# The last four experts of a mixture-of-experts layer: weights of three of them loaded as 4 MB pairs instead of 2 MB chunks

## The chip, the core and the metric

The kernel runs on one core of one Trainium2 chip. The metric is the device time of one execution in microseconds (us); where several executions are compared, their median. One more execution was taken with the hardware profiler: its span and its trace are what is read below.

## The reference

One encoder layer on 256 tokens of 1024 float32 values: a mixing stage (gated linear attention and grouped-query attention side by side), then a mixture of experts, and a final RMS norm. The change touches only how the expert weights come in:

```python
def moe_ffn(x, w_router, b_router, w1, b1, w2, b2):      # top-4 of 32 experts
    ...
    def expert_block(args):
        xb, e = args
        h = (xb @ w1[e] + b1[e]).astype(jnp.float32)      # 1024 -> 2048
        h_glu = jnp.minimum(h[:, :D_FF], SWIGLU_LIMIT)
        h_lin = jnp.clip(h[:, D_FF:], -SWIGLU_LIMIT, SWIGLU_LIMIT)
        act = (h_glu * jax.nn.sigmoid(SWIGLU_ALPHA * h_glu) * (h_lin + 1.0)).astype(xb.dtype)
        return act @ w2[e] + b2[e]                        # 1024 -> 1024
```

Each expert has 8 MB of w1 and 4 MB of w2 in float32, 12 MB in all, and all 32 are read: 384 MB out of 421 MB that the kernel moves.

## The kernel before

**Work.** The experts are taken in order, each for up to 64 of its tokens at a time. The weights of an expert come as six chunks of 2 MB, numbered r = 0 to 5 in the expert: four of w1 (two rows of 128 input features each, by 2048 columns) and two of w2. TensorE works through them in that order. For a chunk of w1 it issues 16 matmuls by the profile's count (line 1696), after the fourth it gathers the rows of the next expert (line 1588), adds the previous expert's result to the output banks (`combine`, line 1607), turns the hidden values (line 1724), the gates (line 1733) and the gathered rows (line 1596), and then does the two chunks of w2 (line 1742, 16 matmuls each) and the bias rows of the next expert (line 1517).

**The ring.** The chunks lie in a ring in SBUF of 8 slots of 2 MB. Both SP, which issues every load, and TensorE count chunks by the semaphore `chunk_used`: SP may load into a slot when the chunk that lay there has been used. All loads go down SP's one queue, in the order in which SP issues them. TensorE waits on a semaphore of the slot (`slot_in`), or of a pair of slots (`pair_in`), before the first matmul of what was loaded.

**Three ways of loading.** Chunks 0 to 71 (twelve experts) are loaded singly, 2 MB each (line 358, function `load`). From chunk 72 on they are loaded by pairs: one transfer of 4 MB into two neighbouring slots (line 401, `load_pair`). SP waits until both slots are free, and TensorE waits for the whole pair ahead of the first of its two chunks. Experts 16 to 27 are done by a loop of bodies of four experts (24 chunks). The last body, experts 28 to 31, is written out behind the loop. Its chunks are called u = 0 to 23 here, its experts q = 0 to 3. Before the change all its chunks are loaded singly again, and of its last expert the chunks r = 3, 4 and 5 (`FINE`) each in two pieces of 1 MB with a semaphore of their own (line 365, `load_pieces`).

**The end.** For the last expert, `last_hidden` turns the hidden values in two halves and does w2 by pieces (lines 1650 and 1656). After that come the last result (ScalarE, line 692), the last `combine`, the norm with `fin_g` (loaded at line 440 into slot 0, once chunk u = 18 has been used) and the stores.

Of the kernel before, what the change touches and what calls it, by code (L numbers as in the profile page):

```python
# [40 lines left out]
EXPERTS, TOP_K, FF = 32, 4, 1024  # L41
# [22 lines left out]
SLOTS = 8  # L64
# [11 lines left out]
FINE = (3, 4, 5)  # L76
# [5 lines left out]
UNROLL = 4  # L82
PER_BODY = UNROLL * PER_EXPERT
PAIR = 2
# [39 lines left out]
def encoder_layer(nc, x, w_in, w_out, w_router, w1, b1, w2, b2, gate_w, columns, rows, final_g,  # L124
                  c_keep, c_front, later, split, out):
    ctx = ExitStack()
    with ctx:
# [3 lines left out]
        def sem(name):  # L131
            return ctx.enter_context(nc.semaphore(name))
# [142 lines left out]
        S = type("Semaphores", (), {n: sem(n) for n in names})  # L275
        win_in = [sem(f"win_in{k}") for k in range(KD)]
        slot_in = [sem(f"slot_in{s}") for s in range(SLOTS)]
# [15 lines left out]
        def slot_of(c):  # L293

            return (c - OUTSIDE + TURN) % SLOTS

        def ring_slot(c):

            return (ring_chunks.index(c) + TURN) % SLOTS

        def earlier_halves(i):
            return sum(1 for o in SOON if o + SLOTS <= i and (o + TURN) % SLOTS == (i + TURN) % SLOTS)

        def slot(s):
            return ring[:, s * SLOT:(s + 1) * SLOT]
# [12 lines left out]
        def _(sp):  # L318
# [37 lines left out]
            def load(to, loaded, e, r):  # L356

                sp.dma_start(to, rows_of(e, r)[:, r % PAIR * SLOT:(r % PAIR + 1) * SLOT]).then_inc(loaded, 16)

            def load_pieces(to, e, r):  # L360

                for i in range(GROUPS):
                    n = SLOT // GROUPS
                    at = r % PAIR * SLOT + i * n
                    sp.dma_start(to[:, i * n:(i + 1) * n], rows_of(e, r)[:, at:at + n]).then_inc(piece_in[FINE.index(r) * GROUPS + i], 16)
# [37 lines left out]
            for i in range(SLOTS, len(ring_chunks)):  # L403
                c, s = ring_chunks[i], ring_slot(ring_chunks[i])
                if i - SLOTS in SOON:
                    e, r = divmod(c, PER_EXPERT)
# [16 lines left out]
            last = rounds * bodies + (bodies - 1)  # L423
            with sp.Fori(WRITTEN, last) as it:
                for u in range(0, PER_BODY, PAIR):
                    q, r = divmod(u, PER_EXPERT)
                    s = slot_of(u)
                    sp.wait_ge(S.chunk_used, it * PER_BODY + (u - SLOTS + PAIR))
                    load_pair(s, (it * UNROLL + q) % EXPERTS, r)
            for u in range(PER_BODY):  # L430
                q, r = divmod(u, PER_EXPERT)
                sp.wait_ge(S.chunk_used, last * PER_BODY + (u - SLOTS + 1))
                if q == UNROLL - 1 and r in FINE:
                    load_pieces(slot(slot_of(u)), EXPERTS - 1, r)
                else:
                    load(slot(slot_of(u)), slot_in[slot_of(u)], EXPERTS - UNROLL + q, r)
# [766 lines left out]
        def _(pe):  # L1203
# [30 lines left out]
            def xT(k, t=None):  # L1234
                return turned[:, k, :] if t is None else turned[:, k, t * P:(t + 1) * P]


            for k in range(KD):
# [4 lines left out]
                def put(o, l, r, first):  # L1243
                    return mm(o, l, r, start=a and first, stop=z, skip_group_check=True)  # L1244
# [3 lines left out]
                def keys_and_queries():  # L1248
                    for i, c0 in enumerate((C_GQ, C_GK)):
                        for pair in range(2):  # L1250
                            last = put(bank[MIX[i]][:, pair * SEQ:(pair + 1) * SEQ], w[:, c0 + pair * P:c0 + (pair + 1) * P], xT(k), pair == 0)
                    return last
# [4 lines left out]
                for banks, c0, c1 in ((ATT_A, C_ZG, C_TAIL), (ATT_B, C_TAIL, D_IN)):  # L1257
                    for t in range(TILES):
                        last = put(bank[banks[t]][:, 0:c1 - c0], xT(k, t), w[:, c0:c1], True)
                        if z:  # L1260
                            last.then_inc(S.pass1, 1)
                if not a:
                    last = keys_and_queries()
# [42 lines left out]
            for k in range(KD):  # L1306
                for t in range(TILES):
                    last = mm(bank[6 + t][:, :], xT(k, t), w_in_sb[:, k, C_GV:C_GR], start=k == 0, stop=k == KD - 1)  # L1308
# [303 lines left out]
            def nth_in_body(u):  # L1612

                return u // SLOTS + 1

            def loaded(q, r, it, final_body):

                u = q * PER_EXPERT + r
                if isinstance(it, int):
                    c = it * PER_BODY + u  # L1620
                    if c in EARLY:
                        i = EARLY.index(c)
                        pe.wait_ge(early_in[i], 16 if i < OUTSIDE - 1 else 16 * W1_ROWS)
                        return early[i] if i < OUTSIDE - 1 else early_rows
                    s = ring_slot(c)
                    if c < PAIRS_FROM:
                        pe.wait_ge(slot_in[s], (ring_chunks.index(c) // SLOTS + 1 + earlier_halves(ring_chunks.index(c))) * 16)
                    elif r % PAIR == 0:
                        pe.wait_ge(pair_in[s // PAIR], ((c - PAIRS_FROM) // SLOTS + 1) * 16)
                    return slot(s)  # L1630
                s = slot_of(u)
                if final_body:
                    singles = (PAIRS_FROM - 1 - OUTSIDE - (s - TURN) % SLOTS) // SLOTS + 1
                    singles += sum(1 for o in SOON if (o + TURN) % SLOTS == s)
                    pe.wait_ge(slot_in[s], (singles + nth_in_body(u)) * 16)
                elif r % PAIR == 0:
                    pe.wait_ge(pair_in[s // PAIR], (it * LOADS_PER_BODY + (nth_in_body(u) - PAIRS_FROM // SLOTS)) * 16)
                return slot(s)
# [38 lines left out]
            def expert(n, q, it, first=False, second=False, rows=None, final=False, final_body=False):  # L1677
# [7 lines left out]
                for c in range(W1_CHUNKS):  # L1685
                    if first and c == W1_CHUNKS // 2:
                        pe.wait_ge(S.xg_ready, 1)
                    fine = final and c in FINE
                    chunk = slot_for(q, c) if fine else loaded(q, c, it, final_body)
                    for r in range(W1_ROWS):  # L1690
                        k = c * W1_ROWS + r
                        if fine:
                            pe.wait_ge(piece_in[FINE.index(c) * GROUPS + r], 16)
                        for j in range(GROUPS):
                            for g in range(2):
                                last = mm(bank[(2, 5)[g]][j * CAP:(j + 1) * CAP, :], xg[:, k * CAP:(k + 1) * CAP],  # L1696
                                          of_group(row_of(chunk, r, 2 * FF), g, j), start=False, stop=k == KD - 1,
                                          skip_group_check=True)
                        if first and c in SOON and r == W1_ROWS // 2 - 1:
                            last.then_inc(S.half_used, 1)  # L1700
                    last.then_inc(S.chunk_used, 1)

                    if first and c == 0:
                        turn_first(1)
                    if first and c == 1:
                        turn_gates()
                    if rows:
                        rows(c)
# [29 lines left out]
                for s in range(W2_CHUNKS):  # L1738
                    chunk = loaded(q, W1_CHUNKS + s, it, final_body)
                    for r in range(W2_ROWS):  # L1740
                        for j in range(GROUPS):
                            last = mm(bank[6][j * CAP:(j + 1) * CAP, :], hidT[:, r, s * CAP:(s + 1) * CAP],  # L1742
                                      row_of(chunk, r, D)[:, j * 512:(j + 1) * 512], start=s == 0 and r == 0,
                                      stop=s == W2_CHUNKS - 1 and r == W2_ROWS - 1, skip_group_check=True)
                        if first and W1_CHUNKS + s in SOON and r == W2_ROWS // 2 - 1:
                            last.then_inc(S.half_used, 1)
                    last.then_inc(S.chunk_used, 1)
# [68 lines left out]
```

## Time and profile before

| | |
|---|---|
| median of 3 runs | 1043.68 us (1043.23 to 1044.42) |
| profiled execution, its time | 1042.15 us |
| its span | 1040.4 us |
| moved by DMA | 420.96 MB, mean 405 GB/s |
| TensorE busy | 998.6 us, 96% |
| VectorE, ScalarE busy | 220.2 us, 133.8 us |
| mean granted TensorE clock | 0.989 of full speed |

The span is what the trace covers; the execution's own time is 1.75 us longer. Matmuls overlap, so TensorE's busy share says little: what counts is when a group of matmuls starts, and what ended the idle time ahead of it. The granted clock has two levels, 1.00 (2.4 GHz) and 0.50 (1.2 GHz); a value between them is a mean over a stretch.

### The profile page before, as it was taken

To read this page: it belongs to the slowest core of one execution; us is meant where nothing else is said; L and a number is where in the kernel's file an instruction comes from. 1 tells how busy PE (TensorE), PEld (TensorE's weight loads), DVE (VectorE), ACT (ScalarE), POOL (GpSimd) and SP (SyncE) were. 2 spreads that over 40 slices of the span, in tenths; PEclk is the share of its full clock that TensorE was granted. 3 is DMA by queue.
4 is the path that set the end of the run, shared out by engine and by line. 5 is a ranking of instruction groups with operands and counts; after the bars stand their busy time and mean duration, and the time that the engine had idled before them with its cause. 6 is when DMAs were issued, how large, how long until landed. Compare 5 with 4: busy or idle time off the path is not lost.

```text
span 1040.4 us, 11246 instructions
## 1 busy us (share of the span) xinstructions
PE 998.6 (96%) x4709; PEld 425.0 (41%) x4709; DVE 220.2 (21%) x517; ACT 133.8 (13%) x267; POOL 12.3 (1%) x18
## 2 busy tenths in 40 slices
PE   9999999999999999989999989999999999999996
PEld 7656444444444444433333334333333333343332
DVE  2595341111111111101111111111111111011112
ACT  1164211111100001101111010001111011001112
POOL 0101000000000000000000000000000000000000
PEclk9999999999999999999999989999999999999999
DMA  9857889999999999999999999999999999999995
GB/s 335 239 220 312 363 312 430 426 428 426 428 428 427 427 428 428 431 433 431 430 430 433 430 431 430 430 431 433 432 433 431 428 433 432 427 426 428 427 424 228
DMA packets 27876, 420.96 MB, mean 405 GB/s; under 512 B 4480, under 2 KB 4992, under 8 KB 7584
## 3 DMA queue, kind: packets, MB, share of 16 engines
q1 hardware_dynamic: 27552, 420.15, 96.0%
q8 instruction: 29, 0.48, 0.2%
q10 hardware_dynamic: 288, 0.27, 0.1%
q14 instruction: 7, 0.06, 0.0%
HBM read 419.36 MB, written 1.05 MB: 404 GB/s over the span
## 4 chain that ended last, share of the span: by engine, by line
PE 64%; DMA 32%; DVE 2%; ACT 1%; issue 0%; SPq 0%; POOL 0%; POOLq 0%
DMA ring<-in_w_dram 32%; PE bank L1696 28%; PE bank L1742 14%; PE bank L1607 4%; PE bank L1244 3%; PE bank L1588 3%; PE bank L1492 1%; PE bank L1323 1%; PE bank L1724 1%; PE bank L1420 1%; PE bank L1596 1%; PE bank L1517 1%; PE bank L1656 1%; PE bank L1308 0%; PE bank L1733 0%
## 5 line engine op out<-in xcount | busy, mean ns | idle before, releaser
L1696 PE MATMUL bank<-ring,work 128*64 128x512 f32 x2000 | 453.5, 605 | 29.9 <-DMA ring<-in_w_dram 29.8
L1696 PEld LDWEIGHTS bank<-ring,work 128*64 128x64 f32 x2000 | 174.7, 138 | 288.8 <-issue 235.2
L1742 PE MATMUL bank<-ring,work 128*64 128x512 f32 x992 | 219.7, 595 | 0.2
L1124 DVE TENSOR_SCALAR work<-bank 128x512 f32<-128x512 f32 x31 | 21.4, 691 | 640.6 <-PE bank L1696 640.6
L1742 PEld LDWEIGHTS bank<-ring,work 128*64 128x64 f32 x992 | 68.7, 137 | 129.5 <-issue 124.5
L655 ACT ACTIVATE bank<-work 128x512 f32<-128x512 f32 x31 | 18.6, 601 | 495.6 <-DVE work L1124 495.6
L1607 PE MATMUL bank<-work 64*128 64x512 f32 x256 | 63.6, 615 | 0.7 <-ACT work L692 0.7
L1588 PE MATMUL bank<-h,work 128*64 128x512 f32 x248 | 60.0, 593 | 0.0
L668 ACT ACTIVATE work<-bank 128x512 f32<-128x512 f32 x31 | 18.5, 597 | 214.5 <-PE bank L1742 214.5
L1607 PEld LDWEIGHTS bank<-work 64*128 64x128 f32 x256 | 22.0, 186 | 41.8 <-issue 40.2
L1094 DVE TENSOR_TENSOR work<-bank,ffn_pairs 128x512 f32<-128x512 f32 x31 | 21.4, 691 | 72.2 <-PE bank L1596 72.2
L1588 PEld LDWEIGHTS bank<-h,work 128*64 128x64 f32 x248 | 23.5, 137 | 30.0 <-issue 30.0
L1724 PEld LDWEIGHTS bank<-ckeep,work 128*128 128x128 f32 x124 | 17.3, 209 | 24.7 <-DVE work L1130 23.2
L650 ACT ACTIVATE work<-bank 128x512 f32<-128x512 f32 x31 | 18.5, 597 | 46.8 <-DVE work L1130 43.6
L1724 PE MATMUL bank<-ckeep,work 128*128 128x128 f32 x124 | 23.2, 309 | 1.1 <-DVE work L1130 1.1
L1244 PE MATMUL bank<-ring,work 128*128 128x416 f32 (+1 forms) x64 | 22.9, 502 | 0.0
L660 ACT ACTIVATE work<-bank 128x512 f32<-128x512 f32 x31 | 18.5, 597 | 28.9 <-PE bank L1724 28.8
L1127 DVE SCALAR_TENSOR_TENSOR work<-work 128x512 f32<-128x512 f32 x31 | 21.5, 692 | 1.1
L1130 DVE TENSOR_TENSOR work<-work,bank 128x512 f32<-128x512 f32 x31 | 21.3, 687 | 1.1
L1125 DVE TENSOR_SCALAR work<-bank 128x512 f32<-128x512 f32 x31 | 21.1, 680 | 0.0
L1517 PE MATMUL bank<-biases,sel 96*64 96x512 bf16 x128 | 20.0, 389 | 0.0
L1596 PE MATMUL bank<-ckeep,work 128*128 128x128 f32 x124 | 20.0, 283 | 0.0
(218 smaller groups left out, 496.8 us busy)
## 6 DMA issues: line engine op xcount, KB each, us to landing
ring<-in_w_dram SPq DMA_DIRECT2D x48, 4096.0 KB, 30.0
ring<-in_w_dram SPq DMA_DIRECT2D x87, 2048.0 KB, 19.8
ring<-in_w_dram SPq DMA_DIRECT2D x12, 1024.0 KB, 20.6
ring<-in_w_in_dram SPq DMA_DIRECT2D x7, 1168.0 KB, 18.1
work<-in_w_dram SPq DMA_DIRECT2D x2, 2048.0 KB, 14.9
ring<-in_w_out_dram SPq DMA_DIRECT2D x2, 1024.0 KB, 10.2
ring<-in_w_out_dram SPq DMA_DIRECT2D x1, 2048.0 KB, 17.0
h<-in_x_dram SPq DMA_DIRECT2D x4, 256.0 KB, 6.4
```

The lines of the kernel that those rows point to most:

```text
L1094: nc.vector.tensor_tensor(xg.rearrange("p (h r c) -> p h r c", h=GROUPS, c=CAP), bank[2][:, :].rearrange("p (r h c) -> p h r c", h=GROUPS, ...
L1124: nc.vector.tensor_scalar(glu, bank[2][:, :], LIMIT, None, ALU.min).then_inc(S.glu_ready, 1)
L1127: nc.vector.scalar_tensor_tensor(lin, lin, 1.0, glu, ALU.add, ALU.mult).then_inc(S.dve_step, 1)
L1130: nc.vector.tensor_tensor(lin, lin, bank[2][:, :], ALU.mult).then_inc(S.hid_ready, 1)
L1244: return mm(o, l, r, start=a and first, stop=z, skip_group_check=True)
L1517: mm(bank[(2, 5)[g]][j * CAP:(j + 1) * CAP, :], sel, of_group(b1_parts, g, j), start=True, stop=False, skip_group_check=True)
L1588: last = mm(bank[6][j * CAP:(j + 1) * CAP, :], onehot[:, t, :], h[:, t, j * 512:(j + 1) * 512], start=t == 0, stop=t == TILES - 1, skip_gr ...
L1596: last = nc.tensor.transpose(bank[2][:, r * P:(r + 1) * P], apart[:, :, r], ident)
L1607: last = mm(bank[Y[i]][:, :], gatedT[j * CAP:(j + 1) * CAP, t, :], res[j * CAP:(j + 1) * CAP, :], start=start, stop=stop, skip_group_check ...
L1696: last = mm(bank[(2, 5)[g]][j * CAP:(j + 1) * CAP, :], xg[:, k * CAP:(k + 1) * CAP], of_group(row_of(chunk, r, 2 * FF), g, j), start=False ...
L1724: last = nc.tensor.transpose(bank[5][:, r * P:(r + 1) * P], apart[:, :, r], ident)
L1742: last = mm(bank[6][j * CAP:(j + 1) * CAP, :], hidT[:, r, s * CAP:(s + 1) * CAP], row_of(chunk, r, D)[:, j * 512:(j + 1) * 512], start=s = ...
```

## The change

For the first three experts of the last body (u = 0 to 17) SP now issues nine transfers of 4 MB instead of eighteen of 2 MB, each when both of its slots are free. TensorE waits for them by the pair's semaphore, ahead of the first chunk of each pair. The last expert (u = 18 to 23) is loaded as before: three single chunks and six pieces. Its count on `slot_in` is adapted, because fewer single loads go ahead of it. Bytes, order of the bytes, places in the ring and all computation stay as they are.

```diff
             for u in range(PER_BODY):
                 q, r = divmod(u, PER_EXPERT)
+                if q < UNROLL - 1:
+                    if r % PAIR == 0:
+                        sp.wait_ge(S.chunk_used, last * PER_BODY + (u - SLOTS + PAIR))
+                        load_pair(slot_of(u), EXPERTS - UNROLL + q, r)
+                    continue
                 sp.wait_ge(S.chunk_used, last * PER_BODY + (u - SLOTS + 1))
-                if q == UNROLL - 1 and r in FINE:
+                if r in FINE:
                     load_pieces(slot(slot_of(u)), EXPERTS - 1, r)
                 else:
                     load(slot(slot_of(u)), slot_in[slot_of(u)], EXPERTS - UNROLL + q, r)
@@
                 s = slot_of(u)
-                if final_body:
+                if final_body and q == UNROLL - 1:
                     singles = (PAIRS_FROM - 1 - OUTSIDE - (s - TURN) % SLOTS) // SLOTS + 1
                     singles += sum(1 for o in SOON if (o + TURN) % SLOTS == s)
-                    pe.wait_ge(slot_in[s], (singles + nth_in_body(u)) * 16)
+                    pe.wait_ge(slot_in[s], (singles + 1) * 16)
                 elif r % PAIR == 0:
                     pe.wait_ge(pair_in[s // PAIR], (it * LOADS_PER_BODY + (nth_in_body(u) - PAIRS_FROM // SLOTS)) * 16)
```

## Rows read from the trace of the kernel before

**Rows 1.** The page: span, and DMA rate in 40 equal slices.
```profile
span 1040.4 us, 11246 instructions
GB/s 335 239 220 312 363 312 430 426 428 426 428 428 427 427 428 428 431 433 431 430 430 433 430 431 430 430 431 433 432 433 431 428 433 432 427 426 428 427 424 228
```

**Rows 2.** The chain that ended last, from 960 us: start us, us, what.
```profile
978.94 34.01 DMA ring<-in_w_dram
...
1024.73 6.18 PE bank L1656 x28
```

**Rows 3.** Windows, loads by pairs and loads by singles: busy time, PEclk, DMA share, GB/s.
```profile
444.00:902.00 458.00, 432.06 (x1980) 168.34 (x1978) 69.02 (x156) 40.60 (x76) 0.00 (x0) 0.98 1.00 431
910.20:998.30 88.10, 85.12 (x407) 34.28 (x404) 16.32 (x36) 10.00 (x19) 0.00 (x0) 1.00 1.01 427
```

**Rows 4.** DMA issues from 850 us on: count, KB each, median us from issue to landing.
```profile
ring<-in_w_dram SPq DMA_DIRECT2D x3, 4096.0 KB, 31.4
ring<-in_w_dram SPq DMA_DIRECT2D x6, 1024.0 KB, 34.1
ring<-in_final_g_dram SPq DMA_DIRECT2D x1, 512.0 KB, 20.7
```

**Rows 5.** Timeline of SP's queue from 860 us: start us, us, what.
```profile
982.46 13.91 SPq L365 DMA_DIRECT2D ring<-in_w_dram  x6
1008.29 0.33 SPq L440 DMA_DIRECT2D ring<-in_final_g_dram  x1
```

**Rows 6.** Timeline of TensorE, last body: start us, us, what, [idle before <- releaser].
```profile
921.74 13.96 PE L1696 MATMUL bank<-ring,work 128*64 128x512 f32 x64
935.47 1.94 PE L1588 MATMUL bank<-h,work 128*64 128x512 f32 x8
...
983.65 3.70 PE L1696 MATMUL bank<-ring,work 128*64 128x512 f32 x16 [1.22 <-DMA ring<-in_w_dram]
988.53 3.70 PE L1696 MATMUL bank<-ring,work 128*64 128x512 f32 x16 [1.17 <-DMA ring<-in_w_dram]
...
997.23 7.09 PE L1742 MATMUL bank<-ring,work 128*64 128x512 f32 x32
...
1004.60 7.19 PE L1696 MATMUL bank<-ring,work 128*64 128x512 f32 x32
1012.99 7.14 PE L1696 MATMUL bank<-ring,work 128*64 128x512 f32 x32 [1.20 <-DMA ring<-in_w_dram]
```

**Rows 7.** Timeline of TensorE while the loads come by pairs.
```profile
461.86 7.14 PE L1696 MATMUL bank<-ring,work 128*64 128x512 f32 x32 [2.51 <-DMA ring<-in_w_dram]
...
608.86 10.07 PE L1696 MATMUL bank<-ring,work 128*64 128x512 f32 x32 [3.06 <-DMA ring<-in_w_dram]
...
842.25 7.14 PE L1696 MATMUL bank<-ring,work 128*64 128x512 f32 x32 [1.03 <-DMA ring<-in_w_dram]
...
854.39 7.09 PE L1742 MATMUL bank<-ring,work 128*64 128x512 f32 x32
...
861.77 7.11 PE L1696 MATMUL bank<-ring,work 128*64 128x512 f32 x32
871.39 7.14 PE L1696 MATMUL bank<-ring,work 128*64 128x512 f32 x32 [2.51 <-DMA ring<-in_w_dram]
...
900.53 8.83 PE L1696 MATMUL bank<-ring,work 128*64 128x512 f32 x32 [2.47 <-DMA ring<-in_w_dram]
...
914.37 7.09 PE L1742 MATMUL bank<-ring,work 128*64 128x512 f32 x32
```

**Rows 8.** The first reader of `fin_g`: durations in ns, first and last start in us.
```profile
L1175 DVE TENSOR_TENSOR tok<-bank,ring x2: 691/691/691, 1033.6 to 1034.6; 128x512 f32<-128x512 f32 x2
```

**Rows 9.** Windows behind three of those waits, columns as in rows 3.
```profile
608.00:614.70 6.70, 5.84 (x14) 1.89 (x16) 0.00 (x0) 0.00 (x0) 0.00 (x0) 0.50 1.01 435
871.40:875.00 3.60, 3.60 (x18) 1.47 (x20) 0.00 (x0) 0.00 (x0) 0.00 (x0) 1.00 1.01 437
901.60:904.80 3.20, 3.20 (x11) 0.86 (x8) 0.00 (x0) 0.00 (x0) 0.00 (x0) 0.50 0.98 420
```

## The prediction

> **What bounds the kernel now.** I read four views, in this order. The page first: from the seventh slice to the last but one, DMA moves 424 to 433 GB/s without a break [rows 1]. The windows say the same more sharply: the DMA engines are fully busy (share 1.00) while the loads come by pairs, and again in the last body, where they come singly [rows 3]. So up to the last loads the kernel goes at the pace of its weights. The reader is to see that this doesn't yet say what ends it. For that there is the chain of waits: it follows a transfer to 1012.95 us, and from there on it is TensorE, with the engines that follow it, until 1040.4 [rows 2]. The timeline of TensorE shows which transfer that is: at 1012.99 the matmuls of u = 20 start, the third chunk of the last expert, after 1.20 us of waiting for it [rows 6]. Of the six pieces behind u = 20 none is on the chain, though DMA is still moving them. The last pair of pieces was issued by 992.6 to 996.4 (the stretch of six issues ends there, the last one long) [rows 5], and by the median of 34.1 us they land around 1027 to 1030 [rows 4]; TensorE runs its 28 matmuls of w2 from 1024.73 in one go [rows 2], at a plain 0.22 us each, so none of them stands waiting.
>
> So the end is set by: landing of u = 20, or the moment when TensorE is done with u = 19, whichever is later, plus 1040.4 - 1012.99 = 27.4 us. Now it is the landing, and TensorE has 1.20 us to spare. That spare time is what the change must be weighed against.
>
> **The change, part by part.** *The transfers.* Six chunks by pairs take one period of the pair stage: TensorE's waits end at 842.25 and 900.53, two experts apart, so 58.28 / 2 = 29.14 us for an expert [rows 7]. Six single chunks take 1012.99 - 983.65 = 29.34 us (u = 14 to u = 20) [rows 6]. The same ratio is in the rates, 431 against 427 GB/s [rows 3]. For three experts that is 3 x 0.20 = 0.6 us, by which everything from u = 18 on lands earlier; u = 20 lands at 1012.95 - 0.6 = 1012.35. Nine issues fewer on SP cost nothing: SP sits waiting for free slots, with 30 us of work in the queue.
>
> The Trainium skill (DMA: Bandwidth & Descriptors, "Anatomy of one DMA — SWDGE (gpsimd) path") gives each transfer a fixed cost of about 2.0 us beside the time of its bytes. By that nine transfers fewer would be worth up to 18 us if they ran one by one, and the forecast would be faster. The trace does not agree for a full queue: 2 x 29.34 / 6 - 29.14 / 3 = 0.07 us a pair.
>
> *SP's wait.* A pair is issued when both slots are free, one chunk later than a single one; queued behind this wait are all later loads and `fin_g`. It costs nothing: a load lies about 31 us in the queue before it has landed, three times the 9.71 us (29.14 / 3) that a pair takes [rows 4], so the queue holds some 20 us of work at each issue. The pair stage, with this very wait, kept the engines at share 1.00 [rows 3]. If that cover were gone, the cost would be at most one chunk, 4.9 us, once.
>
> *TensorE's wait.* This is where I see the cost. With pairs TensorE may start u = 14 only when u = 15 has landed too. Now it starts u = 14 at 983.65 and u = 15 at 988.53, each on its landing, and by the time u = 15 is there only one chunk is left to do [rows 6]. With pairs both start at the landing of the pair. That is 900.53 + 3 x 29.14 = 987.95. (0.6 us ahead of 988.53, as it should be.) From there, all by start-to-start distances of undisturbed rows:
> - from the start of that pair to the first matmul of w2: 854.39 - 842.25 = 12.14 us [rows 7], so 1000.09. Now it is 997.23 [rows 6]: 2.86 us later. The w2 pair has landed long before, at 987.95 + 9.71 = 997.66;
> - from there to u = 18: 1004.60 - 997.23 = 7.37 [rows 6] (7.38 in the pair stage, 861.77 - 854.39 [rows 7]), so 1007.46. u = 18 has landed at about 1002.5;
> - u = 18 and 19 without a wait: half of 935.47 - 921.74 = 13.73 [rows 6], so 6.87, and u = 20 can start at 1014.33.
>
> u = 20 has landed by then (1012.35), and no wait is left: the 1.20 us are used up, and TensorE is late by 1014.33 - 1012.99 = **1.34 us**. The pieces behind come 0.6 us earlier and are asked for 1.3 us later, so they hold up nothing, and the tail is only shifted. `fin_g` is issued when u = 18 is used: 1008.29 now [rows 5], 2.9 us later then. It lands at 1029.0 [rows 4, 5]; shifted by the full 2.9 us it would be there at 1031.9, and its first reader starts at 1033.6 now [rows 8], at 1034.9 then. Everything in experts q = 0 and 1 is within the ring's slack: TensorE waits there in either kernel.
>
> Sum: +1.34. The span becomes 1040.4 + 1.3 = 1041.7, the profiled execution 1042.15 + 1.3 = 1043.5, and the median 1043.68 + 1.34 = **1045.0 us**. (The profiled execution lies 1.5 us under the median. I take the difference as the same for both.) That is +0.13%.
>
> *The clock.* With the pair wait at u = 14 TensorE stands idle ahead of it, and what the clock does there now counts in full, because nothing behind u = 14 waits for DMA any more. In the pair stage eight waits lasted 2.4 us or more, from the one that ended at 461.86 to that at 900.53. After five of them the clock fell to 0.50 (1.2 GHz), three not (the first and the last of the eight [rows 7]; two of the five and one of the three [rows 9]). The cost: from 900.53 to w2 13.84 us instead of 12.14, so 1.7 us; in the longest case, at 608.86, 10.07 instead of 7.14, 2.9 us [rows 7]. After a fall TensorE is late, and the wait of the next expert is short (about 1 us, as the 1.03 at 842.25), after which the clock never fell. So falls come in every second expert at most. The waits of 1.2 us that the kernel before has in its last body brought none, its windows are at 1.00 [rows 3].
>
> What happens at u = 14 (q = 2) then depends on the experts ahead. In this execution the clock fell at 900.53, so q = 0 would wait about 1 us, q = 1 about 2.6, and q = 2 about 1 (clock fell at q = 1) or 2.7. Another execution may stand the other way round. With a fall in five of eight long waits (0.63), and none after a fall, a wait is long in x = 1 - 0.63 x of the cases, so 0.61, and a fall just at u = 14 has 0.61 x 0.63 = 0.38. I cost it at nothing in the likeliest case, with 1.7 us as the other end (2.9 the rare extreme).
>
> The Trainium skill (TensorE: Matmul & The Clock Gate, "HAM oscillation — how this bites in real kernels") says that a wait for DMA between blocks of matmuls drops the clock to half and lets each next block start cold. By that the fall at u = 14 would be certain and the sum 1.34 + 1.7 = +3.0 us. The trace agrees on the price, and on the rule only in five of eight.
>
> **The rivals.**
> - *The clock falls at u = 14.* +1.34 + 1.7 = +3.0 us: 1046.7, slower by 0.29%. For it: five of eight such waits. Against it: the falls alternate, and a fall at q = 1 protects q = 2. It decides from a cost of 0.75 us on (2.09 - 1.34). Chance 0.36.
> - *The landing stays the bound.* The landing of a load is that of its slowest DMA engine. If that falls behind by 1 to 2 us in other executions late in the body, both kernels wait for u = 20 and only the 0.6 us of faster loads are seen: 1043.1. For it: the spare time is small. Against it: three waits in a row end at an even distance, 29.14 us twice (842.25, 871.39, 900.53) [rows 7]. A lag d between u = 15 and u = 20 gives 1.34 - d, down to -0.6 from d = 1.94 on. Chance 0.11.
> - *Loads by pairs are worth more than the rate says*, since the queue is served better. It would have to be 2 us or more in nine transfers, and the pair stage shows 0.6. Chance 0.02.
> - *The queue runs dry between pairs*, up to 4.9 us: 1048.6. Against it: share 1.00 over 458 us of pairs. Chance 0.01.
>
> **How the numbers follow.** A measurement of this kernel can tell about 0.2%, 2.09 us, from no change. The likeliest case, 0.50: TensorE late by 1.3 us, 1045.0, in a range of 1044.3 to 1045.7 (the three runs spread by 0.7 about their median). Same: 0.50 + 0.11 = 0.61, faster 0.02, slower 0.36 + 0.01 = 0.37. The range goes from the landing case (1043.1) to the case of the clock with that spread (1046.7 + 0.7): 1043.0 to 1047.4, outside it mainly the double-length fall (1047.9) and the dry queue.
>
> **What would show it.** Right: in the last body TensorE's groups of line 1696 come as x32 behind a wait; a wait that ends at about 988.0; line 1742 of q = 2 starts at about 1000.1, and from there to the end of line 1696 no wait for the ring at all, with the 1.20 us at u = 20 gone; u = 20 starts about 1014.3; the DMA rate of the last body 431 instead of 427 GB/s, and the last loads 0.6 us earlier. Wrong: a wait still standing at u = 20 (then the landing is the bound, and it may be faster), a clock of 0.50 behind 988 (then +3.0), or a DMA share under 1.00 between 910 and 1000.

## The result and the profile after

| | before | changed |
|---|---|---|
| median of 20 runs each | 1043.14 us (1042.12 to 1044.42) | 1044.66 us (1043.44 to 1046.84) |
| ratio of the times, changed to before, 95% interval | | 1.0019 [1.0013, 1.0025] |
| profiled execution: span, its time | 1040.4, 1042.15 us | 1044.3, 1046.02 us |

The changed kernel is slower by 0.19%, 2.0 us by the ratio and 1.5 us by the medians (the means, 1043.21 and 1045.07, are 1.9 apart). Median and mean differ because its 20 runs are not one heap. Twelve lie between 1043.44 and 1044.80 (median 1044.40, +1.26 us on the median of before), eight between 1045.80 and 1046.84 (median 1046.07, +2.9), and none between. No run of before lies above 1044.42. The profiled execution is one of the eight.

Its page has the same DMA rate as before up to the last two slices:

```profile
span 1044.3 us, 11229 instructions
...
GB/s 348 247 191 313 366 314 429 427 427 429 428 427 428 427 427 429 432 430 432 431 431 431 431 431 430 434 429 434 431 433 431 433 431 433 431 432 430 428 420 160
```

The timeline of TensorE in the last body (line 1701 is 1696 of before, 1747 is 1742, 1612 is 1607):

```profile
930.53 8.83 PE L1701 MATMUL bank<-ring,work 128*64 128x512 f32 x32 [3.01 <-DMA ring<-in_w_dram]
...
959.68 7.14 PE L1701 MATMUL bank<-ring,work 128*64 128x512 f32 x32 [0.85 <-DMA ring<-in_w_dram]
...
988.83 8.77 PE L1701 MATMUL bank<-ring,work 128*64 128x512 f32 x32 [2.52 <-DMA ring<-in_w_dram]
...
1002.68 7.09 PE L1747 MATMUL bank<-ring,work 128*64 128x512 f32 x32
...
1010.05 13.95 PE L1701 MATMUL bank<-ring,work 128*64 128x512 f32 x64
1023.93 1.99 PE L1612 MATMUL bank<-work 64*128 64x512 f32 x8
```

Read it beside [rows 6]. The two single starts of w1 at 983.65 and 988.53 are gone; u = 14 and 15 come as one group of 32 at 988.83, behind a wait of 2.52 us. From there down no row has a wait for the ring, and the 1.20 us ahead of u = 20 have vanished: u = 18 to 21 are one group of 64. The three waits end 29.15 us apart, as in [rows 7].

The windows give the clock and the rate (columns as in [rows 3]):

```profile
910.20:998.30 88.10, 81.72 (x376) 32.20 (x373) 12.05 (x29) 7.40 (x14) 0.00 (x0) 0.96 1.00 430
988.80:992.00 3.20, 3.17 (x8) 1.02 (x9) 0.00 (x0) 0.00 (x0) 0.00 (x0) 0.50 1.00 430
```

The rate of the last body is 430 GB/s, where singles had 427 [rows 3], at DMA share 1.00: the transfers are the better for being paired. The last loads did not come 0.6 us earlier for it, though: by the landing events of the two traces (the time of a load's last one) u = 20 landed at 1013.21, and before at 1012.95. And right behind the start of u = 14 the granted clock is 0.50 (1.2 GHz).

The chain that ended last now leaves the DMA a good 24 us sooner than in [rows 2], at 988.79 and not at 1012.95:

```profile
958.86 29.93 DMA ring<-in_w_dram
...
988.83 8.77 PE bank L1701 x32
...
1002.68 7.09 PE bank L1747 x32
...
1010.22 13.78 PE bank L1701 x64
```

What was said to cost nothing did. `fin_g` is issued and read later than in [rows 5, 8], and the load still lands at 1029.2, 8 us ahead of its first reader (SP's timeline, DMA issues, and the reader's line):

```profile
1013.73 0.33 SPq L445 DMA_DIRECT2D ring<-in_final_g_dram  x1
```

```profile
ring<-in_final_g_dram SPq DMA_DIRECT2D x1, 512.0 KB, 15.5
```

```profile
L1180 DVE TENSOR_TENSOR tok<-bank,ring x2: 691/692/692, 1037.4 to 1038.5; 128x512 f32<-128x512 f32 x2
```

The two profiled spans differ by 3.9 us, and three terms add up to it: the pair u = 14, 15 was waited for until 988.83, 0.9 us later than worked out from the other execution (987.95); TensorE came 2.86 us later to w2 and had 1.52 to spare at u = 20 (1012.99 - 1004.60 - 6.87 by starts; the 1.20 of the row is counted from a modelled end), which leaves 1.34; and from 988.83 to w2 it took 13.85 us in place of 12.14, 1.7. The first I take for a difference between executions, the other two are the change. For this speak the kernels further down that also load u = 14 and 15 singly or as a pair, each in an execution of its own. Singly, u = 15 was waited for until 988.53 (before) and 989.46 (`e9_only_finer_u20`); as a pair until 987.84, 988.48, 988.74 and 988.83. The spread within each way of loading is as large as the 0.9 us.

### The profile page after: what moved, and what is told of

The parts are those of the page before. It is cut to its first block, busy times and chain, and to the rows that moved or that the text cites. A ratio compares the mean times of both kernels' runs of the same rounds, so it can differ in the third digit from the quotient of the medians.

```text
span 1044.3 us, 11229 instructions
## 1 busy us (share of the span) xinstructions
PE 1000.9 (96%) x4709; PEld 426.0 (41%) x4709; DVE 220.1 (21%) x517; ACT 133.8 (13%) x267; POOL 12.2 (1%) x18
## 4 chain that ended last, share of the span: by engine, by line
PE 72%; DMA 24%; DVE 2%; ACT 1%; issue 0%; SPq 0%
PE bank L1701 33%; DMA ring<-in_w_dram 24%; PE bank L1747 16%; PE bank L1612 4%; PE bank L1593 4%; PE bank L1249 3%; PE bank L1729 2%; PE bank L1497 1%; PE bank L1328 1%; PE bank L1425 1%; PE bank L1601 1%; PE bank L1522 1%; PE bank L1661 1%; DMA ring<-in_w_in_dram 1%; PE bank L1313 0%; PE bank L1738 0%
```

## The experiments

All kernels but `e4_filled_waits`, `e4b_half_filled` and `e8_better_filled` only choose otherwise which chunks of the last body come by pairs or in pieces. `PAIRED` lists the even chunk of each pair in the last body (the lines that read it are left out here); a chunk outside it is loaded singly. The changed kernel would be `PAIRED = (0, 2, 4, 6, 8, 10, 12, 14, 16)`, the one before `()`. Three sets were run, each beside its own runs of before. Line numbers shift by a few with each edit: 1701 to 1709 is the matmul of w1, 1747 to 1755 that of w2, 1694 and 1698 the filler.

### Which pairs cost: the third expert, one pair out, one pair in

```diff
-PAIRED = (0, 2, 4, 6, 8, 10, 12, 14, 16)
+PAIRED = (0, 2, 4, 6, 8, 10)                  # e1_third_single
+PAIRED = (0, 2, 4, 6, 8, 10, 12, 16)          # e2_one_pair_single
+PAIRED = (14,)                                # e3_only_one_pair
```

> Only the first two experts of the last body come by pairs (u = 0 to 11), the third (u = 12 to 17) singly again. Theory (TensorE is late because it may start u = 14 only when u = 15 has landed, and nothing behind u = 14 waits for DMA any more): the wait for u = 20 comes back, the landing sets the end, and the two experts by pairs give 2 x 0.2 = 0.4 us: 1043.14 - 0.4 = 1042.7, ratio about 0.9996, no second group of runs near +3. Rival (the pairs themselves cost, in the DMA queue or at SP, about +0.65 us an expert): +0.9 to +1.3, ratio 1.0009 to 1.0012.

Measured: 1042.85 us, before 1043.57; ratio 0.9993 [0.9984, 1.0002], eleven runs from 1042.03 to 1043.66, no second group. Its timeline has the wait for u = 20 back, and the chain that ended last leaves the DMA there again:

```profile
1005.30 7.09 PE L1704 MATMUL bank<-ring,work 128*64 128x512 f32 x32
1013.24 7.14 PE L1704 MATMUL bank<-ring,work 128*64 128x512 f32 x32 [0.85 <-DMA ring<-in_w_dram]
```

> The change, but for one of its nine pairs: u = 14 and 15 are loaded singly. Theory: u = 14 starts at about 983.1 to 983.7, w2 of the third expert at about 997.7 (when the pair u = 16, 17 has landed), u = 18 at about 1005.1, TensorE is done with u = 19 at 1011.9, ahead of the landing of u = 20 at about 1012.4: -0.5 us against the kernel before, ratio about 0.9995, no second group. Rival (the loss is spread over the nine pairs): eight ninths of it stay, +1.8 us, ratio 1.0017.

Measured: 1042.80 us; ratio 0.9994 [0.9985, 1.0003], 1041.91 to 1043.62. Eight of the nine pairs are in it, and nothing of the loss. The rival would have it at 1.0017, outside the interval. Its trace holds something that I had not reckoned with:

```profile
959.22 8.83 PE L1704 MATMUL bank<-ring,work 128*64 128x512 f32 x32 [2.52 <-DMA ring<-in_w_dram]
...
980.43 13.95 PE L1704 MATMUL bank<-ring,work 128*64 128x512 f32 x64
...
999.46 7.09 PE L1750 MATMUL bank<-ring,work 128*64 128x512 f32 x32
...
1006.83 13.95 PE L1704 MATMUL bank<-ring,work 128*64 128x512 f32 x64
```

Here the clock fell one expert earlier, at 959.22 (8.83 us for 32 matmuls). The third expert's w1 then runs 64 matmuls without a wait, w2 starts at 999.46 and not at 997.7, and there is no wait at u = 20 either: it landed at 1013.20 by its landing event, and TensorE came to it at about 1013.7 (1006.83 + 6.87). So a fall at q = 1 can still reach the end, here by about 0.5 us.

> The kernel before, with the one pair u = 14, 15 alone. Theory: nothing comes earlier, so the pair lands at 988.5 as its second chunk does now, u = 14 starts at 988.5, w2 at 1000.7, u = 18 at 1008.0, u = 20 at 1014.9: +1.9 us where the clock stays up, 1045.0, and up to 1.7 more where it falls behind the wait; the wait ahead of u = 14 is long in every run (no pair loads ahead of it, TensorE stands idle some 6 us), so the slow clock should come in most or all runs: +3.6. In any case more than the whole change with its nine pairs. Rival (loss spread over the pairs): one ninth, +0.2.

Measured: 1047.31 us, all five runs between 1046.67 and 1047.91; ratio 1.0037 [1.0024, 1.0051]. That is 3.7 us over its own runs of before (1043.57), where 3.6 was expected. One pair in place of nine costs about twice what the whole change costs. Timeline and windows:

```profile
990.35 9.06 PE L1704 MATMUL bank<-ring,work 128*64 128x512 f32 x32 [6.03 <-DMA ring<-in_w_dram]
...
1004.40 7.09 PE L1750 MATMUL bank<-ring,work 128*64 128x512 f32 x32
...
1011.77 13.95 PE L1704 MATMUL bank<-ring,work 128*64 128x512 f32 x64
```

```profile
985.00:990.30 5.30, 0.00 (x0) 0.00 (x0) 0.00 (x0) 0.00 (x0) 0.00 (x0) 0.73 0.98 417
990.40:994.20 3.80, 3.80 (x10) 1.25 (x12) 0.00 (x0) 0.00 (x0) 0.00 (x0) 0.50 1.03 440
```

The wait is 6.03 us, the clock falls while it lasts (0.73 as the mean of that stretch, 0.50 behind it), and from the start of u = 14 to w2 it is 14.05 us instead of 12.14.

### Are the eight runs near +3 us those with the slow clock?

```diff
                 for c in range(W1_CHUNKS):
+                    if final_body and not final and c == PAIR:
+                        pe.wait_ge(S.gatedT_sb, n)
+                        for _ in range(4):                      # e4b_half_filled: range(2)
+                            mm(bank[7][:, :], ident, h[:, 0, 0:512], start=True, stop=True)
```

> The change, with four 512-column float32 matmuls that nobody reads put ahead of the wait for the second pair of each of the first three experts of the last body (1.7 us of work in a wait of 0.8 to 2.7; the output is the same). Theory (the runs near +3 us are those in which the clock falls behind a long wait at u = 14): TensorE is no longer idle long enough, the granted clock stays at 1.00 in the last body, and only one group of runs is left, at +1.3 us: ratio 1.0012. Rival (the two groups come from something else, such as a DMA engine that falls back): about 8 of 20 runs still near +3, ratio 1.0019 or, with the added work, above it.

Measured: 1047.52 us, ratio 1.0039 [1.0026, 1.0053]. A miss, by a wrong size of mine: the four matmuls take twice what I had put down.

```profile
989.92 3.70 PE L1694 MATMUL bank<-h,ckeep 128*128 128x512 f32 x8
993.55 7.14 PE L1705 MATMUL bank<-ring,work 128*64 128x512 f32 x32
```

```profile
905.00:1030.00 125.00, 124.54 (x565) 50.40 (x561) 20.15 (x45) 11.43 (x23) 0.00 (x0) 1.00 0.97 413
```

With 3.6 us of filler an expert took 30.2 us of TensorE (u = 8 started at 963.39, u = 14 at 993.55), more than the 29.1 us of its loads, so TensorE was late by itself; the clock did stay at 1.00. It says nothing on the two groups, so it was run again with half the filler, in one set with the changed kernel and with a tenth pair.

> As the run with filled waits, with two matmuls in place of four. The first try had a size wrong: four took 3.63 us (3.70 by the profile's row), not 1.7, more than the waits, so TensorE fell behind by about 1 us an expert and started u = 14 at 993.55, while the granted clock stayed at 1.00 over the whole last body. Two take 1.8 us. Theory: the wait at u = 14 (2.5 us) holds them, u = 14 starts on the landing of its pair at about 988, the clock stays at 1.00, one group of runs at +1.3 us (ratio 1.0012), none near +3. Rival (the two groups come from something else): some 4 of 10 runs stay near +3.

Measured: 1044.25 us, before 1042.73; ratio 1.0014 [1.0005, 1.0023]. Timeline and window:

```profile
985.55 1.98 PE L1694 MATMUL bank<-h,ckeep 128*128 128x512 f32 x4
987.84 7.14 PE L1705 MATMUL bank<-ring,work 128*64 128x512 f32 x32 [0.31 <-DMA ring<-in_w_dram]
...
1000.06 7.09 PE L1751 MATMUL bank<-ring,work 128*64 128x512 f32 x32
...
1007.42 13.95 PE L1705 MATMUL bank<-ring,work 128*64 128x512 f32 x64
```

```profile
905.00:1030.00 125.00, 124.06 (x574) 49.75 (x572) 20.57 (x46) 12.41 (x25) 0.00 (x0) 1.00 0.96 411
```

This is the likeliest case of the prediction to a tenth of a microsecond: u = 14 at 987.84 (said 987.95), w2 at 1000.06 (1000.09), u = 18 at 1007.42 (1007.46), span 1041.7 (1041.7). That it fits so closely is in part chance: the wait of the last expert ahead of the body ended at 900.44 in it, as in the trace of before (900.53), while it ended at 900.92 and 901.32 in the two traces of the changed kernel. Of eleven runs one lies above 1045.0 (1045.32), and their mean clocks are 0.988 to 0.991. The counts alone are weak evidence: with a share of 12 in 31, as the changed kernel has it, one or none in eleven would still come up in about 4 of 100 tries, and the interval overlaps with that of the changed kernel in the same set (from 1.0011). What ties the groups to the clock is the traces, below. The median is also 0.2 us over the expected +1.3.

> The changed kernel itself once more, for a second trace and more runs. Theory: two groups of runs again, about +1.3 and +3.0 us against before, four in ten in the upper one; if this profile falls into the lower one, u = 14 starts at about 988.0 behind a short wait or without a fall of the clock, u = 20 at 1014.3 without a wait, and the span is 1041.7 to 1042.0. Rival (another cause of the groups): a profile of the lower group with a slow clock behind 988, or one of the upper without.

Measured: 1044.96 us; ratio 1.0020 [1.0011, 1.0029]. Of eleven runs seven lie at 1044.20 to 1044.99 and four at 1045.49 to 1045.88 (before 1042.73: +1.5 to +2.3, +2.8 to +3.2). The two groups are less clear here than in the first 20 runs: the gap between them is 0.50 us, and there is one of 0.55 us inside the lower one (1044.41 to 1044.96). This time the profile caught the lower group:

```profile
959.61 8.83 PE L1701 MATMUL bank<-ring,work 128*64 128x512 f32 x32 [2.52 <-DMA ring<-in_w_dram]
...
988.74 7.14 PE L1701 MATMUL bank<-ring,work 128*64 128x512 f32 x32 [0.84 <-DMA ring<-in_w_dram]
...
1000.95 7.09 PE L1747 MATMUL bank<-ring,work 128*64 128x512 f32 x32
...
1008.32 13.95 PE L1701 MATMUL bank<-ring,work 128*64 128x512 f32 x64
```

```profile
960.50:963.70 3.20, 3.20 (x10) 1.07 (x8) 0.00 (x0) 0.00 (x0) 0.00 (x0) 0.50 1.00 430
988.80:992.00 3.20, 3.20 (x16) 1.30 (x17) 0.00 (x0) 0.00 (x0) 0.00 (x0) 1.00 0.96 415
```

The clock fell at q = 1, which made the wait at u = 14 short (0.84 us), and there it stayed up: 12.21 us from u = 14 to w2, against 13.85 in the other trace of the same kernel. The landings of the two stand within 0.1 us (988.74, 988.83), and the spans are 1042.6 and 1044.3: the 1.7 us between these two executions are the slow clock. Its span is 0.6 us over the upper end that I had set, since its loads land 0.8 us later than those that I had worked from.

### A tenth pair

```diff
-PAIRED = (0, 2, 4, 6, 8, 10, 12, 14, 16)
+PAIRED = (0, 2, 4, 6, 8, 10, 12, 14, 16, 18)
```

> The change and a tenth pair, u = 18 and 19. By itself such a pair would let u = 18 start 3.4 us later. Theory: behind u = 14 TensorE is late anyway; the pair lands at 997.66 + 9.71 = 1007.4 and TensorE comes to u = 18 at 1007.5, so the tenth pair costs nothing (0 to 0.2 us): the same two groups as the change, +1.3 and +3.0, ratio 1.0019. Rival (each pair costs its share, or each pair in front of the end costs one chunk's time): +0.2, or up to +3.4 on top.

Measured: 1044.05 us; ratio 1.0017 [1.0007, 1.0026], six runs from 1043.55 to 1044.05 and five from 1044.97 to 1045.54. No slower than the changed kernel in the same set (1.0020). Here the mean clock of the whole execution goes with the group, 0.987 to 0.988 in the lower and 0.984 to 0.985 in the upper; in the 20 runs of the changed kernel it does not separate them (0.985 to 0.989 in both), where falls elsewhere in the kernel count as well (the two traces of it have eight and seven from 440 us on). The profiled execution is of the upper group, and u = 18 stands behind no wait:

```profile
988.48 8.60 PE L1704 MATMUL bank<-ring,work 128*64 128x512 f32 x32 [2.51 <-DMA ring<-in_w_dram]
...
1009.52 13.96 PE L1704 MATMUL bank<-ring,work 128*64 128x512 f32 x64
```

From the start of u = 14 to w2 it took 13.67 us. So of the four traces in which all nine pairs were loaded and TensorE waited for u = 14, the two of the upper group (the changed kernel's first and this one) have the slow clock behind it, and the other two (the changed kernel's second and the filled one) do not. And a wait costs nothing where TensorE comes too late for it anyway.

### Towards a better version

```diff
-FINE = (3, 4, 5)
+FINE = (3, 4, 5, 2)      # u = 20 in two pieces too; its two semaphores are early_in[0:2], waited for to 32
```

`e9_only_finer_u20` has this with `PAIRED = ()`, `e6_better` and `e6b_better_again` with all pairs but u = 14, 15. `e8_better_filled` adds the two filler matmuls in the first two experts (`final_body and q < 2 and c == PAIR`).

> The change with u = 14, 15 singly, and the chunk r = 2 of the last expert (u = 20) in two pieces of 1 MB as well. Theory: with TensorE in time the landing of u = 20 sets the end; in pieces its first half lands 2.4 us ahead, and the bound passes to the last piece of u = 21, at about 1017.9 - 0.5, plus 1.7 us of matmuls: end of w1 at about 1019.2 instead of 1020.1. Sum against the kernel before: -0.5 and -0.4, ratio 0.9990. Rival (the tail behind u = 20 is bound elsewhere, by the hidden values or w2's pieces): only the -0.5 of the kernel with one pair single.

Measured: 1042.29 us, before 1042.73; 0.9994 [0.9985, 1.0003]. That is what the kernel with one pair single had without the pieces, so the rival fits as well as the theory.

> The kernel with u = 14, 15 singly and u = 20 in pieces, with two filler matmuls ahead of the second pair's wait in the first two experts of the last body. In the trace of the kernel with one pair single, the clock fell at the second expert (959.24) and TensorE, 1.7 us late from there, was at u = 20 only at 1013.7, with no wait left: so a fall one expert earlier takes part of the gain. Theory: the filler prevents it, and the sum of -0.5 and -0.4 comes out in every run: ratio 0.9991, with fewer runs above the median than without the filler. Rival (the fall one expert earlier is within the slack): same as without the filler.

Measured: 1042.27 us, before 1043.23; 0.9991 [0.9982, 1.0000], eleven runs from 1041.67 to 1042.74. Its timeline:

```profile
957.06 1.98 PE L1698 MATMUL bank<-h,ckeep 128*128 128x512 f32 x4
959.63 7.14 PE L1709 MATMUL bank<-ring,work 128*64 128x512 f32 x32 [0.59 <-DMA ring<-in_w_dram]
...
998.55 7.09 PE L1755 MATMUL bank<-ring,work 128*64 128x512 f32 x32 [0.40 <-DMA ring<-in_w_dram]
1005.93 14.29 PE L1709 MATMUL bank<-ring,work 128*64 128x512 f32 x64
```

> The kernel before, all singles in the last body, with only u = 20 in two pieces. Theory: the bound passes to the last piece of u = 21 (landed at 1017.9) plus 1.7 us: -0.4 us, ratio 0.9996. Rival: nothing, 1.0000.

Measured: 1043.05 us; 1.0001 [0.9992, 1.0010].

```profile
1005.53 10.66 PE L1705 MATMUL bank<-ring,work 128*64 128x512 f32 x48
1016.50 1.94 PE L1705 MATMUL bank<-ring,work 128*64 128x512 f32 x8 [0.30 <-DMA ring<-in_w_dram]
1018.98 1.94 PE L1705 MATMUL bank<-ring,work 128*64 128x512 f32 x8 [0.54 <-DMA ring<-in_w_dram]
```

The bound did pass to the pieces of u = 21, as the waits show, but no gain is seen: the expected 0.4 us (0.9996) and none at all both lie in this interval.

> The kernel with u = 14, 15 singly and u = 20 in pieces once more, beside its filled version. Expected the same as in its first run, -0.4 to -0.9 us, ratio 0.9991 to 0.9996.

Measured: 1042.85 us; 0.9997 [0.9988, 1.0006].

All kernels of this section lie below the changed kernel: `e6_better` does so in one set with it (up to 1.0003 against from 1.0011), the others by intervals of different sets (up to 1.0010 at most against from 1.0013). None is shown to beat the kernel before: the best of them, 0.9991, has an interval that ends just at 1. In `e8_better_filled` the wait has moved to the pair u = 16, 17 (998.55), as in both runs without the filler (997.79 and 997.83), and from there TensorE runs through to the end without one, so there the finer u = 20 had nothing to give.

## Why the prediction was right

- **What sets the end.** Right. The chain left the DMA at u = 20 before and leaves it at u = 14 now; with the whole third expert single again it comes back to u = 20 (`e1_third_single`, 0.85 us). With only u = 14, 15 single it leaves the DMA at u = 8 behind the slow clock there (`e2_one_pair_single`, 959.18), or at the pair u = 16, 17 (`e6_better`, `e8_better_filled`).
- **The transfers.** Right by rate and period: 430 against 427 GB/s, 29.15 us for a paired expert against 29.34. The sign that the last loads come 0.6 us earlier was not seen: u = 20 landed at 1013.21 and 1013.15 in the two traces of the changed kernel, at 1012.95 before. From execution to execution the landings differ by more than that. Where u = 15 came singly it was waited for until 988.53 or 989.46, and the pair of the experiment that loads only it by a pair until 990.35. The 0.6 us can't be spent anyway, because nothing waits for a landing behind u = 14. Where it could, in the kernels with u = 14, 15 single, the ratios are 0.9993 and 0.9994; each interval also holds 1, so this gain is likely, not shown.
- **TensorE's wait, +1.34 us.** Right, though the text called 1.20 us the spare time and the sum used the 1.52 by starts. The lower group came at +1.26 us (+1.5 to +2.3 in the second set) and the filled kernel showed the steps at 987.84, 1000.06 and 1007.42. One pair out of nine carries it: without that one the loss is gone, with that one alone it is larger than the change's.
- **The clock.** The rival at +3.0 us with chance 0.36 turned out to be no rival but the other part of the runs: eight of 20, at +2.9. It was worked out as a chance for an execution and used as a chance for the median; for a kernel that is timed many times it is a share of the runs, and the ratio comes out between both, 1.0019. So the likeliest case, 1045.0, was near the median (1044.66), and the ratio at the very edge of what I called the same. Luck had a part in it. The base of the sum, 1043.68, was the median of three runs and 0.54 us above that of 20 (1043.14); with that base the likeliest case would be 1044.5, 0.2 us under the measured median and not 0.3 over it. And the median stayed in the lower group only because fewer than half of the runs had the fall. That the profiled execution lies under the median by the same amount in both kernels was wrong too: 1.0 us before, and within 0.1 us of the median of its own group in both sets of the changed kernel (in the second set 1044.31 against 1044.33).
- **The chance of a fall behind a long wait** was put at 0.63 from eight waits. In the 13 traces of this study, 77 of 96 waits of 2.4 to 3.1 us had one, 0.80. By the same step, 0.80 / 1.80 = 0.44 for a fall at u = 14; seen were 12 of 31 runs, by the times. That the clock never falls twice in a row is not quite so either (an exception stands in the last section). As for the certain fall that the prediction drew from the Trainium skill (TensorE: Matmul & The Clock Gate, "HAM oscillation — how this bites in real kernels"): that section describes waits of about 3 to 5 us. For waits of 2.5 us "certain" was a step of my own, and the traces do not bear it out.
- **The landing as the bound** (0.11): seen in neither trace of the changed kernel, though its pair landed up to 0.9 us later than worked out. What it needed was a lag between u = 15 and u = 20. By the landing events these two were 24.47 us apart before, 24.42 and 24.45 in the two traces of the changed kernel, 24.74 in the filled one. So the lag is there from before u = 14 on, where it delays either kernel alike.
- **The dry queue and the fixed cost of a transfer:** neither. DMA share 1.00 in the last body; nine transfers fewer gained 0.6 us by the periods. The 18 us were an estimate from the fixed cost of about 2.0 us that the Trainium skill gives for one transfer (DMA: Bandwidth & Descriptors, "Anatomy of one DMA — SWDGE (gpsimd) path"); with a full queue no run here shows it.

What stays open: what a fall at q = 1 costs the kernels with u = 14, 15 single (about 0.5 us in one trace, and `e6_better` beside `e8_better_filled` is within the noise), and why one filled run in eleven came at 1045.32 with a mean clock of 0.991. The kernel before has such runs too, three in 101 over the four sets (1045.42, 1045.55 and 1045.85), and no trace of one was taken.

## What to carry to other kernels

When two loads are merged, their consumer may start only when the second has landed: compare that delay (here 2.86 us) with the time to spare at the wait that ends last (1.52 us), and stop merging before the last stretch in which the consumer still waits for loads. A stall that a later load hides in the middle of a kernel, and the slow clock behind it, cost in full near the end. A chance that differs from execution to execution is a share of the runs, and moves the mean by that share of its price.

## What the runs showed of the hardware

- Behind a wait of TensorE of 2.4 to 3.1 us the granted clock fell from 2.4 to 1.2 GHz in 77 of 96 cases, behind 116 waits under 1.6 us never (13 traces, from 440 us on). Of seven waits of 3.4 to 3.7 us five had one. A fall mostly cost 1.4 to 1.7 us, 1.9 behind the wait of 6.03 us, and twice 2.9 to 3.0. Since it shortens the next wait it protects the next expert: but for one case, falls came in every second expert at most. The exception, where a late load kept the next wait at 2.27 us, is in the second trace of the changed kernel:

```profile
608.49 8.83 PE L1701 MATMUL bank<-ring,work 128*64 128x512 f32 x32 [2.64 <-DMA ring<-in_w_dram]
...
639.06 8.83 PE L1701 MATMUL bank<-ring,work 128*64 128x512 f32 x32 [2.27 <-DMA ring<-in_w_dram]
```

- Whether the expert that matters is an even or an odd one in that sequence changes from execution to execution of one program (two traces of the changed kernel). So its runs fall into two groups about 1.7 us apart, and a profile shows one of them only.
- The 16 increments by which a load reports its landing drift apart over the kernel. Between 110 and 140 us the first and the last of a load were 0.4 to 0.8 us apart in eleven of the 13 traces (1.1 and 2.6 in the other two), for the weight loads behind 980 us 4.9 to 7.2 us in all (landing events). TensorE started on the last one: for u = 20 of before it stands at 1012.95, and the matmuls start at 1012.99.
- A matmul of 512 float32 columns against a full 128 x 128 float32 tile took 0.45 us for each of its two records (3.63 us for eight), twice the 0.22 us of one with 64 stationary columns: this was the mis-sized filler. No run isolates the reason. A tile of 64 x 128 took 0.24 us a record in `combine` (line 1607, 1.92 us from start to start for eight), so the number of columns alone is not it.
